# Attention's last heads and the first merge panel of a two-layer decoder kernel: the merge panel's GLA half is woven between the heads

## The reference

```python
q, k, v, qi, ki, wi, gq, gk, gv, la, gr, ga, gb = split(rms_norm(x) @ w_in)
attn_o = top-k masked softmax attention(q, k, v)      # 8 heads, 4 blocks of 128 prompt queries
gla_o  = gated linear attention(gq, gk, gv, la)       # 4 heads
g_out  = rms_norm(gla_o) * silu(gr)
merged = sigmoid(ga) * (attn_o @ w_oa) + sigmoid(gb) * (g_out @ w_ob)
x      = x + merged @ w_o
x      = x + (silu(gate) * up) @ w_down               # feed-forward
```

## Time and profile before

| | |
|---|---|
| device time, median of 3 runs | 1821.06 us (1820.52, 1821.06, 1824.76) |
| the profiled execution: device time | 1819.51 us |
| the profiled execution: span of the trace | 1817.7 us |
| mean granted clock of PE | 0.991 of full speed |
| layer 0: first head's logits to last `attn_pv` | 337.50 to 414.84 us |
| layer 0: from there to the end of `oab0` | 414.84 to 425.65 us |
| layer 1: the same two stretches | 1233.78 to 1309.56, and to 1320.38 us |

### The profile page before, as it was taken

The page is one execution under the profiler, slowest core; times in us unless marked ns, Lnnn a source line. Parts: engine busy times, 40 slices in busy tenths (PEclk is TensorE's granted clock), DMA queues, the critical chain, the costliest instruction groups (busy, mean ns, idle before and its releaser), DMA issues.

```text
span 1817.7 us, 33285 instructions
## 1 busy us (share of the span) xinstructions
PE 1741.4 (96%) x12738; PEld 1632.9 (90%) x12738; DVE 1098.8 (60%) x2146; ACT 794.8 (44%) x1535; POOL 783.0 (43%) x510
## 2 busy tenths in 40 slices
PE   7998999999999999999999999999999999999998
PEld 6886888788999999999987868877899999999998
DVE  3765786465587537627537658645557873574463
ACT  4442214564566426426534332136644662463352
POOL 2323442432446446536333333425234564563452
PEclk9999999999999999999999999999999999999999
DMA  4232224214223413413123222351233233233122
GB/s 155 67 88 64 64 64 135 75 36 122 77 82 94 116 57 99 116 50 88 50 77 82 61 74 72 75 144 41 70 105 95 59 103 106 71 94 111 49 60 79
DMA packets 263303, 151.06 MB, mean 83 GB/s; under 512 B 15910, under 2 KB 255594, under 8 KB 263146
## 3 DMA queue, kind: packets, MB, share of 16 engines
q1 hardware_dynamic: 263146, 148.94, 29.5%
HBM read 141.53 MB, written 7.37 MB: 82 GB/s over the span
## 4 chain that ended last, share of the span: by engine, by line
PE 75%; DVE 16%; ACT 4%; issue 3%; POOL 1%; DMA 0%; SPq 0%; DVEq 0%; ACTq 0%; POOLq 0%
PE prod L1458 33%; PE prod L1512 8%; PE prod L1513 8%; PE prod L1514 8%; PE prod L1402 2%; PE prod L1403 2%; PE prod L1404 2%; DVE scores L2803 2%; DVE top L2801 1%; PE aux L1869 1%; PE aux L1857 1%; DVE in_lo L2364 1%; PE aux L1630 1%; PE aux L1832 1%; DVE aux L2611 1%
## 5 line engine op out<-in xcount | busy, mean ns | idle before, releaser
L1893 POOL TENSOR_TENSOR w_lo<-w_raw,w_hi 128x1024 fp32r<-128x1024 f32 (+2 forms) x160 | 370.0, 2312 | 741.7 <-ACT w_hi L1994 737.2
L1994 ACT ACTIVATE w_hi<-w_raw 128x1024 fp32r<-128x1024 f32 (+2 forms) x160 | 163.0, 1019 | 275.6 <-PE prod L1458 244.0
L1458 PE MATMUL prod<-in_hi,w_hi 128*128 128x288 f32 x1024 | 236.8, 313 | 7.3 <-DVE in_lo L2364 6.2
L1458 PE MATMUL prod<-in_hi,w_lo 128*128 128x288 f32 x1024 | 222.9, 300 | 0.0
L1458 PE MATMUL prod<-in_lo,w_hi 128*128 128x288 f32 x1024 | 222.6, 300 | 0.0
L1512 PE MATMUL prod<-t_hi,ff_hi 128*128 128x288 f32 x704 | 208.6, 296 | 1.2 <-ACT in_sum L2048 0.6
L1458 PE MATMUL prod<-mid_hi,w_hi 128*128 128x288 f32 x960 | 207.6, 298 | 2.1 <-DVE mid_lo L2364 2.1
L1513 PE MATMUL prod<-t_lo,ff_hi 128*128 128x288 f32 x704 | 207.9, 295 | 0.0
L1514 PE MATMUL prod<-t_hi,ff_lo 128*128 128x288 f32 x704 | 207.1, 294 | 0.0
L1458 PE MATMUL prod<-mid_lo,w_hi 128*128 128x288 f32 x960 | 206.3, 296 | 0.0
L1458 PE MATMUL prod<-mid_hi,w_lo 128*128 128x288 f32 x960 | 206.3, 296 | 0.0
(11 more groups left out here) (332 smaller groups left out, 3689.6 us busy)
## 6 DMA issues: line engine op xcount, KB each, us to landing
w_raw<-in_w_in SPq DMA_DIRECT2D x72, 512.0 KB, 3.9
ff_gate<-in_w_ffn_gu SPq DMA_DIRECT2D x44, 512.0 KB, 5.1
ff_up<-in_w_ffn_gu SPq DMA_DIRECT2D x44, 512.0 KB, 3.9
w_raw<-in_w_ffn_down SPq DMA_DIRECT2D x32, 512.0 KB, 3.8
w_raw<-in_w_o SPq DMA_DIRECT2D x16, 512.0 KB, 3.8
w_raw<-in_w_ffn_down SPq DMA_DIRECT2D x16, 384.0 KB, 3.3
k_pages<-in_cache_k SPq DMA_DIRECT2D x32, 128.0 KB, 2.1
v_pages<-in_cache_v SPq DMA_DIRECT2D x32, 128.0 KB, 2.1
```

The lines of the kernel that those rows point to most:

```text
L1458: ins = e.matmul(slot(g)[:, h, :], w[:, slot_w, i * P:(i + 1) * P], a[:, i, h * HALF:(h + 1) * HALF], start=first, stop=last)
L1893: e.tensor_tensor(w_lo[:, p % 2, 0:n], w_raw[:, p % RAW_RING, 0:n], w_hi[:, p % 2, 0:n].bitcast(F32), ALU.subtract).then_inc(w_lo_done, 1)
L1994: e.activation(w_hi[:, p % 2, 0:n], w_raw[:, p % RAW_RING, 0:n], ACT.Copy).then_inc(w_hi_done, 1)
```

## The change

Three things are done, in both layers. `woven` takes four more parts, those of `oab0`'s GLA half; `kept=3` leaves three of them behind the last item, so 81 parts are dealt out among the items and three follow. The GLA slices of `in_hi` and `in_lo` are made one by one beside the parts of `gtb7` (`mix_high`, `mix_low`); a slice of `in_hi` is overwritten once `gtb7` has read it (semaphore `in_read`). And the logits, maxima, exponentials and first scaling of heads 0 and 1 become an item of their own, `heads`, with weight 2.5, ahead of `attn(0, 0)`; the weights now sum to 69.5.

```diff
-FILL = {..., "attn": 1.0, "attn_pv": 0.4, "attn_t": 0.2,
+FILL = {..., "attn": 1.0, "attn_pv": 0.4, "attn_t": 0.2, "heads": 2.5,
...
+    def mix_high(self, kt):
+        self.split(("mix", kt))
+        self.add("mix_high", kt)
+
-    def woven(self, panels, items):
+    def woven(self, panels, items, merged=None, kept=0):
...
-        done, due, total = 0, 0.0, len(panels) * KD
+        parts = [(p, i) for p in panels for i in range(KD)]
+        if merged is not None:
+            parts += [(merged, i) for i in range(4)]
+        done, due, total = 0, 0.0, len(parts) - kept
         for n in range(len(items) + 1):
-            while done < (total if n == len(items) else round(due)):
-                p, i = panels[done // KD], done % KD
+            while done < (len(parts) if n == len(items) else round(due)):
+                p, i = parts[done]
                 if i == 0:
                     self.start(p)
                 self.add("part", p, i)
+                if merged is not None and p == merged - 1:
+                    if 2 <= i < 6:
+                        self.mix_high(i - 2)
+                    if 3 <= i < 7:
+                        self.add("mix_low", i - 3)
...
+        items.append([("heads",)])
         for j, h in order:
             items.append([("attn", j, h)])
...
-        self.woven(range(split, first["oab"]), items)
-        for kt in range(KD):
-            self.split(("mix", kt))
-        self.add("mix", "gla")
-        self.add("mix", "attention")
+        self.woven(range(split, first["oab"]), items, first["oab"], 3)
+        for kt in range(4, KD):
+            self.mix_high(kt)
+            self.add("mix_low", kt)
...
+                    elif (kind, idx) == ("gtb", KD - 1) and i < 4:
+                        ins.then_inc(in_read, 1)
...
+                    elif kind == "heads":
+                        logits(0)
+                        logits(1)
                     elif kind == "attn":
...
-                        if n == 0:
-                            logits(0)
-                            logits(1)
                         e.wait_ge(p_scaled, nth(n + 1, len(ORDER)))
...
+                    elif kind == "mix_high":
+                        kt = step[1]
+                        if kt < 4:
+                            e.wait_ge(in_read, nth(kt + 1, 4))
+                            e.wait_ge(gnorm_done, nth(kt + 1, GH))
+                            e.activation(in_hi[:, kt, :], gla_o[:, kt, :], ACT.Copy).then_inc(split_hi, 1)
                         else:
-                            e.wait_ge(free(("so",)), emptied(("so",)))
-                            e.wait_ge(free(("o", 3)), emptied(("o", 3)))
+                            if kt == 4:
+                                e.wait_ge(ready(last_group("gtb")), filled(last_group("gtb")))
+                                e.wait_ge(free(("so",)), emptied(("so",)))
+                                e.wait_ge(free(("o", 3)), emptied(("o", 3)))
+                            e.activation(in_hi[:, kt, :], attn_t[:, kt - 4, :], ACT.Copy).then_inc(split_hi, 1)
...
-                    elif kind == "mix":
-                        for kt in range(4) if step[1] == "gla" else range(4, KD):
-                            src = gla_o[:, kt, :] if kt < 4 else attn_t[:, kt - 4, :]
-                            low_part(("mix", kt), in_lo[:, kt, :], src, in_hi[:, kt, :])
+                    elif kind == "mix_low":
+                        kt = step[1]
+                        src = gla_o[:, kt, :] if kt < 4 else attn_t[:, kt - 4, :]
+                        low_part(("mix", kt), in_lo[:, kt, :], src, in_hi[:, kt, :])
```

More of the change, by code:

```diff
@@ L82 @@
 Y_STORES = {3: 0, 6: 4, 7: 7}
-FILL = {"intra": 2.0, "intra_out": 1.5, "kv": 1.0, "sround": 2.0, "attn": 1.0, "attn_pv": 0.4, "attn_t": 0.2,
+FILL = {"intra": 2.0, "intra_out": 1.5, "kv": 1.0, "sround": 2.0, "attn": 1.0, "attn_pv": 0.4, "attn_t": 0.2, "heads": 2.5,
         "topk": 0.5, "kcT": 1.0, "slog": 2.4, "gnorm": 2.0}
@@ L593, in build_layer @@
                 self.ff_part(idx[0], p)
-            self.start(p)
+            if p > first["oab"]:
+                self.start(p)
             for step in closing:
@@ L597, in build_layer @@
             closing = []
-            for i in range(KD):
+            for i in range(4 if p == first["oab"] else 0, KD):
                 self.add("part", p, i)
@@ L665, in extra_step @@
             self.open(("so",), 3)
+        if kind == "heads":
+            for i in range(2):
+                self.open(("log",) + self.attn_order[i], i)
         if kind == "attn":
@@ L669, in extra_step @@
             n = order.index((j, h))
-            if n == 0:
-                self.open(("log",) + order[0], 0)
-                self.open(("log",) + order[1], 1)
             self.open(("pT", j, h), 2)
@@ L869, in build @@
         x_filled = semaphore("x_filled")
+        in_read = semaphore("in_read")
         bank_ready = [semaphore(f"bank{i}_ready") for i in range(6)]
@@ L2248, in body @@
                         e.activation(root, root, ACT.Exp, scale=-0.5).then_inc(gn_root, 1)
-                    elif kind == "mix":
[L2251 to L2255, removed]
-                        else:
-                            e.wait_ge(free(("so",)), emptied(("so",)))
-                            e.wait_ge(free(("o", 3)), emptied(("o", 3)))
-                            for kt in range(4, KD):
-                                e.activation(in_hi[:, kt, :], attn_t[:, kt - 4, :], ACT.Copy).then_inc(split_hi, 1)
+                    elif kind == "mix_high":
[4 more added lines that the diff above has]
+                            e.activation(in_hi[:, kt, :], gla_o[:, kt, :], ACT.Copy).then_inc(split_hi, 1)
+                        else:
+                            if kt == 4:
[3 more added lines that the diff above has]
+                            e.activation(in_hi[:, kt, :], attn_t[:, kt - 4, :], ACT.Copy).then_inc(split_hi, 1)
                     elif kind == "kT":
@@ L2314, in body @@
                         e.activation(dst, src, ACT.Copy).then_inc(qk_hi_done, 1)
+                    elif kind == "heads":
+                        e.wait_ge(ready(("spT", 3)), filled(("spT", 3)))
+                        exp_head(0)
+                        exp_head(1)
                     elif kind == "attn":
@@ L2318, in body @@
                         L = (j + 1) * P
[L2319 to L2322, removed]
                         e.wait_ge(ready(("pT", j, h)), filled(("pT", j, h)))
@@ L2903, in body @@
                         e.wait_ge(free(("spT", i)), emptied(("spT", i)))
+                    elif kind == "heads":
+                        max_head(0)
+                        max_head(1)
+                        scale_head(0)
                     elif kind == "attn":
@@ L2907, in body @@
                         L = (j + 1) * P
[L2908 to L2911, removed]
                         if n + 1 < len(ORDER):
```

## The result

The changed kernel takes 1816.82 us (median of 8 runs, 1814.20 to 1820.77), the kernel before 1821.45 us beside it: a ratio of 0.9978 with an interval of 0.9968 to 0.9987, 4.6 us or 0.22% less. It is faster than before, but by about half of what was forecast, and within the 0.3% that the prediction took for no change. (One execution of the kernel before, beside the last three experiments, was in a slower state at 3485.82 us and counts in no ratio.)

What follows compares the result with a forecast made beforehand. PE, busy 96% of the span, bounds the kernel, so gains come from its waits and lower clock: 1817.7 - 2 x (2.05 + 0.85 + 0.2) - 1.6 = 1809.9 us span, median put at 1812.5, range 1807 to 1819.

Steps and rivals of the forecast that it cites:

- Transition: From the transposes of `attn(3, 4)` to the end of `oab0`: 17.95 us, 2.05 us gained in each layer.
- The rival that the hole only moves: Transition still ends with `attn_t`, `in_hi`, `in_lo`; it gains 0.5 and the rest 1.0 a layer: 1817 us, chance 0.17.
- First head: Holes at head 0's logits and first scaling: 1.78 us becomes 0.95, 0.85 gained in each layer.
- Between: PE's waits in the heads behind the first: 2.4 us against 2.6, 0.2 gained in each layer.
- the 1.2: Behind `attn(1, 6)`, PE waits 1.2 us for `pT_t` behind ACT's exponential and weight copy; named the worst new wait.
- the 0.25: Between the heads, a transpose was to wait 0.25 us.
- the 0.2: Between the heads, the logits of block 1 were to wait some 0.2 us for POOL.
- one 0.4: Between the heads, one of two further `attn_pv` was to wait 0.4 us.
- the 0.35: Between the heads, the other of two further `attn_pv` was to wait 0.35 us.
- The clock: Two drops of PE's clock in layer 0 cost 3.3 us; half, 1.6 us, taken back.
- Slower: Rival: weight copies hit an `attn_pv` at all six places of a layer, 7.2 us of holes; 1824.5 us, chance 0.05.
- The chance of 0.68: Chance given to the whole kernel being faster by over 0.3%, under 1815.6 us.

Runs made afterwards that it cites:

- sigmoids_later: Changed kernel with the first merge panel's table load and two sigmoids behind the split of its input on ACT; 1813.12 us, 0.9952 of the kernel before.
- from_gtb4: Changed kernel with the weight splits of panels gtb4 to gtb7 held until behind the next `attn_pv` or part 5 of the panel ahead; 1815.81 us, 0.9959 of before.
- merge_and_sigmoids: Changed kernel without the `heads` item, and with the first merge panel's sigmoids behind its input's split; 1818.89 us, 0.9981 of the kernel before.

## Why the prediction was right and wrong

The forecast was 1812.5 us, 8.6 under before; the sum had 6.2 us of PE's waits and 1.6 of clock, and 0.8 came from how the profiled execution was set against the median. Measured were 4.6. By its steps:

- **Transition**, 2.05 a layer: right. 18.15 us from the transposes of `attn(3, 4)` to the end of `oab0` instead of 17.95 (the sum there gives 2.07, not 2.05); holes of 0.59 and 1.56 instead of 0.1, 0.9 and 1.35. That is 1.9 a layer. No gap stood behind the table load, and `sigmoids_later` shows that load and sigmoids were the whole hole. The rival that the hole only moves fell.
- **First head**, 0.85 a layer: half right. The wait for `k_lo` was 0.85 as worked out, but the 0.1 left for POOL's `w_lo` in the way of the scaling was 0.37: 1.78 became 1.22, a gain of 0.56. I had named the mechanism and the weight split that does it, and not looked up what a blocked scaling costs.
- **Between**, "2.4 against 2.6: 0.2 gained in each layer": this is the step that failed. The waits between the heads are 4.05 us in layer 1 (2.57 in `attn_pv`, 1.07 and 0.41), and were 2.8: 1.25 lost in each layer instead of 0.2 gained, 2.9 of the 3.8 us by which the sum of the waits fell short. I had laid the new places of six weight copies against undisturbed durations of ACT. Of the places named, the 1.2 was 0.97 and one 0.4 was 0.43, but the 0.25 was 1.07, the 0.2 was 0.41, the 0.35 was 0.83, and one of 0.34 I had not seen. At the 1.07, half of what was missed, DVE was late already, because POOL's `q_split` had held its scaling for 1.22 us; the copy then comes on top of that delay. At the 0.83 no scaling was held: the weight copy followed two others of ACT. `from_gtb4` shows that the order of the weight splits sets a good part of those waits (4.05 became 2.57 with the parts dealt out as before), not that it sets all: the 1.07 and the 0.41 stayed. The sign that I had named for being wrong, `pT_t` waits of over 3.5 us a layer, came: 4.3, the transition's 0.59 with them.
- **The clock**, 1.6 in all: not contradicted, and not shown. The waits give 2 x (1.9 + 0.56 - 1.25) = 2.4 us of the 4.6 measured; some 2 us are left for the clock, but by the interval of the ratio (2.4 to 5.8 us) that rest can be anything from 0 to 3.4. In the profiled sections three falls became none, one of which had cost nothing. This execution of the changed kernel had its falls elsewhere, so its span shows nothing of it, and the mean clocks of all runs (0.9896 before in 67, 0.9902 after in 8) differ less than 8 runs can settle.
- **Slower**, the weight copies at all six places: its mechanism, weight copies ahead of a `pT_t` that PE waits for, is a good part of what ate the gain, at 4.3 us of `pT_t` waits instead of the 5.5 from which it decides. That the time lies in the range is no merit of the sum: the range had room for a lost term of 2.9 us. The chance of 0.68 for more than 0.3% had not.

## What to carry to other kernels

When a planner deals work out by weights, any change of the weights moves everything that is tied to the dealt pieces, here six weight splits on two engines. Lay each of those out anew with the engines' real lateness, and cost an operation of VectorE beside a GpSimd one by when the GpSimd one ends, not by its mean. An order that keeps a long copy out from between an exponential and the copy that TensorE waits for was worth as much in the kernel before (4.2 us, with the GpSimd half of the split moved too) as the whole change, and about 1 us by the medians on top of the change. Work that nobody waits for yet (the sigmoids, with their table load) belongs behind work that TensorE waits for (2.8 us of waits in two layers). But hold nothing back before you know when it is due.

## What the runs showed of the hardware

**A scaling on DVE can wait for a whole operation of POOL.** `TENSOR_SCALAR` on 128x128 fp32 took 0.29 us and, if POOL had begun first, 1.22, 1.72 or 1.77 us, each time ending 0.07 or 0.08 us after POOL's did; in the changed kernel's first head:

```profile
1235.95 2.40 POOL L1909 TENSOR_TENSOR w_lo<-w_raw,w_hi 128x1024 fp32r<-128x1024 f32 x1 [1.05 <-issue]
...
1236.71 1.72 DVE L2426 TENSOR_SCALAR p_t<-p_t,p_inv 128x128 f32<-128x128 f32 x1
```

Wider scalings that began behind POOL's `w_lo` ended later after it, as if their own work came last: in before 0.15 us later with 256 columns (1.92 us long), 0.22 with 384 and 0.29 with 512. The maxima beside them, which read PSUM, kept their 0.28 to 0.30 us. The Trainium skill, SBUF — State Buffer, section "SBUF: two separate sides", says that the port pair shared by the two engines is an exclusive lock between a GpSimd operation and a VectorE one that runs in a two-port mode or has two inputs in SBUF: whichever begins first has it for its whole instruction and the other blocks. The traces agree for scalings that began second; which mode they ran in no trace shows.

**The clock fell at long waits.** In the sections of the 13 profiled kernels the clock fell 20 times. Fifteen falls began within 1.4 us of the end of a PE wait of 1.78 to 2.22 us, and there were 20 such waits; four go with one of the 24 waits of 1.36 to 1.72 us (two began behind it, two 0.3 to 0.4 us before it ended), and one came behind two shorter ones, of 0.65 and 1.19 us. A layer's section had 128.9 to 129.7 us of PE work without a fall, and 130.2 to 130.8 in eleven of the twelve with one (129.9 in the other); 3.5 us at a mean clock of 0.51, as in the row of `merge_and_sigmoids` above, are 1.7 us of work lost. Which of the long waits is followed by a fall differs from layer to layer in one execution, and why I can't say.
